# Attention of a hybrid decoder layer: heads in pairs, plain transposes, and the row sum divided out after the value product

## The chip, the cores and the metric

The kernel runs on one core of one Trainium2 chip. The metric is the device time of one execution, in microseconds (us). TensorE multiplies, VectorE (DVE), ScalarE (ACT) and GpSimd (POOL) do the element-wise work, SyncE (SP) issues most transfers.

## The reference

One decoder layer over 16 meta tokens and 1024 tokens of width 1024, all in float32. One input projection feeds two mixers: group A, eight heads of 64 channels with sparse attention, and group B, four heads of gated DeltaNet. Both outputs are gated, concatenated and projected into the residual. The part that the change touches is the attention of group A:

```python
idx_score = jnp.where(causal[None], idx_score, -jnp.inf)
_, sel = lax.top_k(idx_score, topk)               # 256 keys of each query
...
bias = rel_table[_t5_bucket(q_pos[None, :, None] - sel)]
logits = (jnp.einsum('bqhd,bqkhd->bqhk', qb, kg).astype(jnp.float32) * scale
          + jnp.moveaxis(bias, -1, 2).astype(jnp.float32))
logits = jnp.where(valid[:, :, None, :], logits, -jnp.inf)
p = jax.nn.softmax(logits, axis=-1).astype(vg.dtype)
return jnp.einsum('bqhk,bqkhd->bqhd', p, vg)
...
o_attn = _dsa_mixer(...) * jax.nn.silu(z_attn)
```

The kernel doesn't gather: it adds -1e30 to the logits of keys that aren't selected.

## The kernel before

It is written without a scheduler: each engine has its own program, and the engines meet only at semaphores. The stages, in time: projections and norms to about 100 us, index scores to 129, key/query norms and gates to 294, and the convolution's projections on TensorE to 462, while VectorE searches the top 256 keys until 490. Then comes the attention, from 495.8 to about 869, and last the DeltaNet with the output projection (L1453 to L1546; the first L1546 starts at 969 us), to the end of the span.

The attention works through 8 blocks `i` of 128 queries and, in each, 8 heads; `n = 8 i + h` counts them to 64. Block `i` has `KEYS[i] = 16 + 128 (i + 1)` keys, in `i + 2` tiles (tile 0 holds the 16 meta tokens). A head passes through:

- `dots(n)`, L1387 (and L1392 for the meta keys of the last block): queries times keys. Head `h` lies on rows 0 to 63 of the array when it is even and on rows 64 to 127 when it is odd. The logits go to one of two regions of three PSUM banks.
- `logits(n)`, L1028 to L1042 on VectorE: adds the penalty (far keys, L1033) or penalty and bias (near keys, L1039; the sum is prepared on GpSimd, L573), takes the row maximum, and negates it (L1042).
- `probabilities(n)`, L763 on ScalarE: the exponential in place, with its row sum.
- `sums(n)`, L1068 and L1070 on VectorE: the reciprocal of the row sum, and the identity scaled by it, a diagonal matrix.
- `turn_p(n)`, L1405: each tile of probabilities is multiplied by the diagonal as an ordinary matmul, which turns and normalises it. `copy_round` (L342 to L344) brings rounds of up to four tiles to SBUF, on VectorE and ScalarE by turns.
- `weigh(n)`, L1417: values (64 columns, stationary) times turned probabilities, summed over the tiles in bank 5. An even head fills PSUM partitions 0 to 63, an odd head 64 to 127.
- `gate_block(i)`, L1061: after eight heads, the output times the gate `zA`.

TensorE's order is `dots(n)`, `turn_p(n - 2)`, `weigh(n - 3)`; from n = 26 on, every third head is followed by L1433, eight products with one output column each, that sum squares for the DeltaNet (nine times). VectorE's order is `logits(m)`, `sums(m - 1)`, even copies of `m - 2` in the first 32 heads, and with `logits` after the copies in the last 32. A float32 matmul shows as two records in the trace, a float32 transpose (`turn(...)`, as in L1453) as one.

## Time and profile before

| | |
|---|---|
| runs | 1250.92 us median of 3 (1238.6 to 1269.38) |
| profiled execution, span | 1265.9 us; its time outside the span isn't listed |
| TensorE busy | 1155.0 us, 91% |
| VectorE busy | 722.8 us, 57% |
| ScalarE busy | 400.4 us, 32% |
| GpSimd busy | 237.3 us, 19% |
| mean granted clock of TensorE | 0.867 of full speed |
| HBM traffic | 36 GB/s over the span, up to 131 GB/s in a fortieth of it |

Busy time is what an engine spent in its instructions. TensorE's instructions overlap in the array, so its busy time says where it had work, not how fast it was; the spacing of its records says that. A granted clock of 0.50 is 1.2 GHz, 1.00 is 2.4 GHz.

### The profile page before, as it was taken

To read this page: it belongs to the slowest core of one execution; us is meant where nothing else is said; L and a number is where in the kernel's file an instruction comes from. 1 tells how busy PE (TensorE), PEld (TensorE's weight loads), DVE (VectorE), ACT (ScalarE), POOL (GpSimd) and SP (SyncE) were. 2 spreads that over 40 slices of the span, in tenths; PEclk is the share of its full clock that TensorE was granted. 3 is DMA by queue.
4 is the path that set the end of the run, shared out by engine and by line. 5 is a ranking of instruction groups with operands and counts; after the bars stand their busy time and mean duration, and the time that the engine had idled before them with its cause. 6 is when DMAs were issued, how large, how long until landed. Compare 5 with 4: busy or idle time off the path is not lost.

```text
span 1265.9 us, 14746 instructions
## 1 busy us (share of the span) xinstructions
PE 1155.0 (91%) x5008; PEld 762.5 (60%) x5008; DVE 722.8 (57%) x1767; ACT 400.4 (32%) x1237; POOL 237.3 (19%) x257
## 2 busy tenths in 40 slices
PE   6998999989999962999999999996869989999897
PEld 2544344445666631556677776775858867777754
DVE  2436898889999998443334434545365454644422
ACT  3425576694555512311112222332021210300200
POOL 5000000001545511111122121102123031221210
PEclk9989899999999985555569879999577979979999
DMA  4310303002011003000000000002000101101110
GB/s 131 128 49 1 124 26 100 33 17 84 1 67 39 28 1 116 17 12 6 17 1 18 17 1 17 10 1 75 1 1 1 50 1 50 50 1 50 50 50 34
DMA packets 26706, 46.75 MB, mean 37 GB/s; under 512 B 3408, under 2 KB 10864, under 8 KB 26640
## 3 DMA queue, kind: packets, MB, share of 16 engines
q1 hardware_dynamic: 26096, 45.78, 10.7%
q8 instruction: 40, 0.66, 0.2%
q0 software_dynamic: 544, 0.10, 0.2%
q14 instruction: 26, 0.21, 0.1%
HBM read 33.82 MB, written 12.05 MB: 36 GB/s over the span
## 4 chain that ended last, share of the span: by engine, by line
PE 61%; DVE 19%; issue 17%; ACT 2%; SPq 1%; DMA 0%; DVEq 0%; POOL 0%; POOLq 0%
PE ps L1405 10%; PE ps L1417 9%; PE ps L1546 8%; PE ps L1387 8%; PE ps L1252 5%; PE ps L1479 3%; DVE junk L961 3%; PE ps L1490 3%; DVE scores L1154 2%; PE ps L1482 2%; PE ps L1302 2%; PE ps L1433 1%; PE ps L1459 1%; DVE iw L956 1%; DVE iw L971 1%
## 5 line engine op out<-in xcount | busy, mean ns | idle before, releaser
L961 DVE TENSOR_SCALAR_CACHE_REDUCE junk<-scores,iw 128x272 bf16<-128x272 f32 (+6 forms) x224 | 200.6, 896 | 8.0
L1372 PE MATMUL ps<-areaH,areaW 128*128 128x384 f32 (+1 forms) x576 | 168.1, 455 | 1.6 <-ACT areaQ L721 1.6
L1372 PEld LDWEIGHTS ps<-areaH,areaW 128*128 128x128 f32 x576 | 109.4, 190 | 59.9 <-issue 1.8
L1387 PE MATMUL ps<-areaQ 64*128 64x512 f32 (+3 forms) x208 | 105.5, 632 | 34.4 <-ACT areaC L743 33.3
L1405 PE MATMUL ps<-areaH 128*128 128x128 f32 (+1 forms) x704 | 133.1, 340 | 1.3 <-DVE areaH L1070 0.8
L1405 PEld LDWEIGHTS ps<-areaH 128*128 128x128 f32 (+1 forms) x704 | 96.6, 211 | 49.6 <-issue 41.4
L1417 PE MATMUL ps<-areaH,areaQ 128*64 128x128 f32 (+1 forms) x704 | 123.8, 325 | 0.0
L1546 PE MATMUL ps<-areaW,areaQ 128*128 128x512 f32 x256 | 119.7, 613 | 1.7 <-DVE areaQ L1220 1.1
L1417 PEld LDWEIGHTS ps<-areaH,areaQ 128*64 128x64 f32 (+1 forms) x704 | 88.0, 159 | 27.1 <-issue 23.4
L763 ACT ACTIVATE areaH<-areaH,small 128x144 f32<-128x144 f32 (+7 forms) x64 | 50.5, 788 | 154.7 <-DVE small L1042 154.7
L557 POOL TENSOR_TENSOR staging<-staging,areaC 128x520 f32<-128x520 f32 x60 | 75.1, 1285 | 70.4 <-ACT areaC L757 70.4
L1387 PEld LDWEIGHTS ps<-areaQ 64*128 64x128 f32 x208 | 43.1, 239 | 73.3 <-issue 36.6
L573 POOL TENSOR_TENSOR areaH<-scores,tmp 128x256 f32<-128x256 f32 (+1 forms) x64 | 44.5, 696 | 227.0 <-DVE small L1039 221.9
L1546 PEld LDWEIGHTS ps<-areaW,areaQ 128*128 128x128 f32 x256 | 48.4, 198 | 51.6 <-issue 49.9
L1033 DVE CUSTOM_DVE_ANT_0 areaH<-ps,scores 128x16 f32<-128x16 f32 (+5 forms) x48 | 23.8, 497 | 76.6 <-PE ps L1387 76.6
L1252 PE MATMUL ps<-areaW,areaH 128*128 128x460 f32 (+1 forms) x144 | 59.8, 570 | 5.1 <-DMA areaW<-in_w_in 5.1
L811 ACT COPY scores<-ps 128x128 f32<-128x128 f32 x35 | 9.3, 266 | 166.2 <-PE ps L1479 166.2
L1350 PE MATMUL ps<-areaH,areaW 128*128 128x512 f32 x128 | 56.3, 594 | 0.0
L1350 PE MATMUL ps<-areaW,areaH 128*128 128x512 f32 x128 | 56.2, 592 | 0.0
L342 DVE COPY areaH<-ps 16x128 f32<-16x128 f32 x48 | 13.3, 278 | 71.7 <-PE ps L1405 71.3
L344 ACT COPY areaH<-ps 128x128 f32<-128x128 f32 (+3 forms) x40 | 17.0, 426 | 110.7 <-PE ps L1405 107.6
L757 ACT ACTIVATE areaC<-areaC,small 128x520 f32<-128x520 f32 x60 | 42.5, 723 | 24.3 <-POOL staging L557 24.3
(250 smaller groups left out, 1803.4 us busy)
## 6 DMA issues: line engine op xcount, KB each, us to landing
areaW<-in_w_in SPq DMA_DIRECT2D x5, 2048.0 KB, 8.8
areaC<-in_x SPq DMA_DIRECT2D x8, 512.0 KB, 3.5
areaW<-in_w_out SPq DMA_DIRECT2D x2, 2048.0 KB, 8.1
areaQ<-in_x SPq DMA_DIRECT2D x8, 512.0 KB, 5.1
y<-areaQ SPq DMA_DIRECT2D x8, 512.0 KB, 2.6
gate_a_scratch<-staging SPq DMA_DIRECT2D x8, 256.0 KB, 2.3
gate_g_scratch<-staging SPq DMA_DIRECT2D x8, 256.0 KB, 2.0
areaH<-gate_a_scratch SPq DMA_DIRECT2D x8, 256.0 KB, 2.9
```

The costliest lines, as they stand in the source:

```text
L557: nc.gpsimd.tensor_tensor(sums, sums, prod, ALU.add).then_inc(s_cvP, 1)
L573: nc.gpsimd.tensor_tensor(mbn[:, n % 2, 0:near], scores[:, SC0[i + 1] - near:SC0[i + 1]], bias[:, h, 256 - near:256], ALU.add).then_inc(s_ ...
L757: A(half(k)[1], conv[:, m, lo:lo + H2], ACT.Copy, scale=cw[:, 1 + k // 2, m:m + 1]).then_inc(s_prod, 1)
L763: A(L[:, n % 3, 0:nk], L[:, n % 3, 0:nk], ACT.Exp, bias=nm[:, n:n + 1], accum_out=rs[:, n:n + 1]).then_inc(s_P, 1)
L961: V.tensor_scalar(junk[:, 0:KEYS[i]], scores[:, SC0[i]:SC0[i] + KEYS[i]], patf[:, i - 1:i], 0.0, ALU.is_ge, ALU.add, accum_out=cnt[:, i - ...
L1252: ins = mm(ps[0:n, b, 0:NA], hT[:, k, tok(t)], wslot[:, 0, k, 0:NA], start=k == 0, stop=k == KD - 1)
L1350: ins = mm(ps[:, 2 + n % 2, :], w, hh, start=k == 0, stop=k == KD - 1)
L1372: ins = mm(ps[:, n % 4, 0:hi - lo], wslot[:, g % 2, k, 128 * m:128 * m + 128], hT[:, k, lo:hi], start=k == 0, stop=k == KD - 1)
L1387: ins = mm(pf[:, 1536 * (n % 2) + lo:1536 * (n % 2) + hi], qT[r, h // 2, 128 * i:128 * i + 128], kT[r, h // 2, lo0 + lo:lo0 + hi], start=T ...
L1405: ins = mm(ps[0:ROWS[kt], 6 + rr % 2, 128 * j:128 * j + 128], L[:, n % 3, tok(kt)], diag[:, n % 2, :], start=True, stop=True)
L1417: ins = mm(o, vN[0:ROWS[kt], kt, DA * h:DA * h + DA], pT[0:ROWS[kt], n % 2, kt, :], start=kt == 0, stop=kt == i + 1)
L1546: ins = mm(ps[:, 6 + q // 2, :], y, wslot[:, q // 2, k, :], start=k == 0, stop=k == 7)
```

## The change

- `dots(p)` computes a pair of heads (an even one and the next) in one step; the matmuls of the two row halves alternate. Each head writes its own two PSUM banks; up to 400 keys two pairs alternate inside them, above that the next pair waits until VectorE has read all of this one.
- Penalties, bias and queries are negated, so that the row minimum is the exponential's bias as it stands: the negation (L1042) is gone.
- `turn_p` becomes `turn_group`: a plain transpose against the identity, up to four tiles of the pair at a time, two pairs after `dots`. Value products follow two groups later, alternating between the pair's column halves. Groups, sums of squares and some small products share a ring of banks 5 to 7.
- `sums` is gone. Once per block, one reciprocal takes eight row sums, `scale_rows(i)` spreads them over 128 partitions with eight small matmuls, and VectorE multiplies the gate by them; `gate_block(i)` multiplies as before.
- The second half of the output weights (`load_group(7)`) is loaded after the attention, since its place holds four of the attention's buffers.

```diff
-        L = a.take(3, T)
-        pT = a.take(2, NT, 128)
+        L = a.take(6, T)
+        pT = a.take(4, 4, 128)
+        a = Area(areaW[:, KD * 512:2 * KD * 512])
         sqk = a.take(D)
-        mbn = a.take(2, 256)
+        mbn = a.take(4, 256)
         zA = a.take(2, 512)
-        diag = a.take(2, 128)
+        Lm = a.take(HA, META)
...
+        NP = HA * NB // 2
+        HP = HA // 2
+        LAG = 2
+
+        def tiles_of(i):
+
+            full = [(par, kt) for kt in range(1, i + 2) for par in range(2)] + [(0, 0), (1, 0)]
+            return [full[j:j + 4] for j in range(0, len(full), 4)]
+
+        GRP = [(p, tiles) for p in range(NP) for tiles in tiles_of(p // HP)]
+        G0 = [sum(len(tiles_of(q // HP)) for q in range(p)) for p in range(NP + 1)]
+        SQP = 13
+
+        def ring_steps():
+
+            by_step, nxt = [], 0
+            for st in range(NP + LAG):
+                now = []
+                if st == HP * (NB - 1):
+                    now += [("meta", 0, "D"), ("meta", 1, "D")]
+                if SQP <= st < SQP + NT:
+                    now.append(("ssq", st - SQP, "D"))
+                if st >= LAG:
+                    p = st - LAG
+                    for k in range(G0[p], G0[p + 1]):
+                        now.append(("turn", k, "DA"[nxt % 2]))
+                        nxt += 1
+                    if p % HP == HP - 1:
+                        now.append(("scale", p // HP, "D"))
+                by_step.append(now)
+            return by_step
+
+        RING = ring_steps()
+        FLAT = [e for now in RING for e in now]
+        AT_RING = {e[:2]: c for c, e in enumerate(FLAT)}
...
+        def ring_bank(c):
+            return 5 + c % 3
...
+        def logit_base(p):
+
+            return 512 * (p % 2) if KEYS[p // HP] <= 512 else 0
...
-            load_group(7)
+            sp.wait_ge(s_ch, 36)
...
+            load_group(7)
...
-                A(L[:, n % 3, 0:nk], L[:, n % 3, 0:nk], ACT.Exp, bias=nm[:, n:n + 1],
+                nk, buf = KEYS[n // HA], 2 * (n // 2 % 3) + n % 2
+                act.wait_ge(s_red, n + 1)
+                A(L[:, buf, 0:nk], L[:, buf, 0:nk], ACT.Exp, bias=mx[:, n, 1:2], scale=-1.0,
...
+                else:
+                    dve.wait_ge(s_za[k % 2], 16 * (k // 2 + 1))
+                    V.tensor_tensor(zA[:, k % 2, :], bank, zA[:, k % 2, :], ALU.mult).then_inc(s_rd, 1)
...
+            for step in range(NP + LAG):
+                ops = logit_ops(step) if step < NP else []
+                if ops:
+                    dve.wait_ge(s_S, step + 1)
+                    if step >= 3:
+                        dve.wait_ge(s_ring, AT_RING["turn", G0[step - 2] - 1] + 1)
...
+                if step >= LAG and (step - LAG) % HP == HP - 1:
+                    i = (step - LAG) // HP
+                    dve.wait_ge(s_P, HA * (i + 1))
+                    V.reciprocal(rinv[:, i % 2, :], rs[:, HA * i:HA * i + HA]).then_inc(s_ri, 1)
+                if ops:
+                    logits(*ops.pop(0))
+                for what, k, who in RING[step]:
+                    if who == "D" and what != "meta":
+                        read_ring(what, k)
+                    if what == "turn" and k in GATE_AT:
+                        gate_block(GATE_AT[k])
+                    if ops:
+                        logits(*ops.pop(0))
+                while ops:
+                    logits(*ops.pop(0))
+                if 1 <= step < CONV:
+                    conv_tap(11, step)
...
+            def fill(what, k):
+                c = AT_RING[what, k]
+                if c >= 3:
+                    pe.wait_ge(*ring_read(c - 3))
+                return ring_bank(c)
+
+            def dots(p):
+                i, g = p // HP, p % HP
+                lo0, base = split(i), logit_base(p)
+                if KEYS[i] > 512 and p:
+                    pe.wait_ge(s_red, 2 * p)
+                elif p >= 2:
+                    pe.wait_ge(s_red, 2 * (p - 1))
                 for lo, hi in pieces(KEYS[i] - lo0):
-                    ins = mm(pf[:, 1536 * (n % 2) + lo:1536 * (n % 2) + hi], qT[r, h // 2, 128 * i:128 * i + 128],
-                             kT[r, h // 2, lo0 + lo:lo0 + hi], start=True, stop=True)
-                if lo0:
-                    if h:
-                        pe.wait_ge(s_meta, h)
-                    ins = mm(ps[:, 2, 0:META], qT[r, h // 2, 128 * i:128 * i + 128], kT[r, h // 2, 0:META],
+                    for par in range(2):
+                        r = slice(64 * par, 64 * par + 64)
+                        ins = mm(pf[:, 1024 * par + base + lo:1024 * par + base + hi],
+                                 qT[r, g, 128 * i:128 * i + 128], kT[r, g, lo0 + lo:lo0 + hi], start=True, stop=True)
+                ins.then_inc(s_S, 1)
+
...
-                ins.then_inc(s_S, 1)
-
-            def turn_p(n):
-
-                i = n // HA
-                pe.wait_ge(s_dg, n + 1)
-                for r, tiles in enumerate(rounds(i)):
-                    rr = ROUND0[n] + r
-                    if rr >= 2:
-                        pe.wait_ge(*turned(rr - 2))
-                    for j, kt in enumerate(tiles):
-                        ins = mm(ps[0:ROWS[kt], 6 + rr % 2, 128 * j:128 * j + 128], L[:, n % 3, tok(kt)],
-                                 diag[:, n % 2, :], start=True, stop=True)
-                    ins.then_inc(s_PT, 1)
-
-            def weigh(n):
-                i, h = n // HA, n % HA
-                if h == 0 and i:
+                ins.then_inc(s_ring, 1)
+
+            def turn_group(k):
+
+                p, tiles = GRP[k]
+                pe.wait_ge(s_P, 2 * (p + 1))
+                b = fill("turn", k)
+                for j, (par, kt) in enumerate(tiles):
+                    ins = turn(ps[0:ROWS[kt], b, 128 * j:128 * j + 128], L[:, 2 * (p % 3) + par, tok(kt)], ident)
+                ins.then_inc(s_ring, 1)
+
+            def weigh(k):
+                p, tiles = GRP[k]
+                i, g = p // HP, p % HP
+                if i and k == G0[HP * i]:
                     pe.wait_ge(s_on, i)
-                for r, tiles in enumerate(rounds(i)):
-                    pe.wait_ge(*turned(ROUND0[n] + r))
-                    for kt in tiles:
-                        o = ps[DA * (h % 2):DA * (h % 2) + DA, 5, 128 * (h // 2):128 * (h // 2) + 128]
-                        ins = mm(o, vN[0:ROWS[kt], kt, DA * h:DA * h + DA], pT[0:ROWS[kt], n % 2, kt, :],
-                                 start=kt == 0, stop=kt == i + 1)
+                pe.wait_ge(*ring_read(AT_RING["turn", k]))
+                for j, (par, kt) in enumerate(tiles):
+                    h = 2 * g + par
+                    ins = mm(ps[DA * par:DA * par + DA, 4, 128 * g:128 * g + 128],
+                             vN[0:ROWS[kt], kt, DA * h:DA * h + DA], pT[0:ROWS[kt], k % 4, j, :],
+                             start=kt == 1, stop=kt == 0)
                 ins.then_inc(s_o, 1)
 
-            for n in range(HA * NB + 3):
-                if n < HA * NB:
-                    dots(n)
-                if 2 <= n < HA * NB + 2:
-                    turn_p(n - 2)
-                if n >= 3:
-                    weigh(n - 3)
...
+            def scale_rows(i):
+
+                pe.wait_ge(s_ri, i + 1)
+                b = fill("scale", i)
+                for g in range(HP):
+                    for par in range(2):
+                        h = 2 * g + par
+                        ins = mm(ps[DA * par:DA * par + DA, b, 128 * g:128 * g + 128],
+                                 rinv[:, i % 2, h:h + 1].broadcast_to([128, DA]), ident, start=True, stop=True)
+                ins.then_inc(s_ring, 1)
+
+            for step in range(NP + LAG):
+                for what, k, _ in RING[step]:
+                    if what == "meta":
+                        dots_meta(k)
+                if step < NP:
+                    dots(step)
+                for what, k, _ in RING[step]:
+                    if what == "ssq":
+                        sum_squares(k)
+                    elif what == "turn":
+                        turn_group(k)
+                        if k >= 2:
+                            weigh(k - 2)
+                    elif what == "scale":
+                        scale_rows(k)
+            for k in range(len(GRP) - 2, len(GRP)):
+                weigh(k)
```

## Rows read from the trace of the kernel before

**Rows 1.** The page's section 4, the chain that ended last, by engine and line.

```profile
PE 61%; DVE 19%; issue 17%; ACT 2%; SPq 1%; DMA 0%; DVEq 0%; POOL 0%; POOLq 0%
PE ps L1405 10%; PE ps L1417 9%; PE ps L1546 8%; PE ps L1387 8%; PE ps L1252 5%; PE ps L1479 3%; DVE junk L961 3%; PE ps L1490 3%; DVE scores L1154 2%; PE ps L1482 2%; PE ps L1302 2%; PE ps L1433 1%; PE ps L1459 1%; DVE iw L956 1%; DVE iw L971 1%
```

**Rows 2.** Windows of 20 us in the attention: busy of each engine, granted clock.

```profile
core 0: us, PE busy (x) PEld busy (x) DVE busy (x) ACT busy (x) POOL busy (x), PEclk, DMA share, GB/s
...
600.00:620.00 20.00, 20.00 (x79) 12.91 (x78) 6.89 (x27) 3.10 (x10) 3.80 (x4) 0.50 0.08 27
...
640.00:660.00 20.00, 20.00 (x98) 14.60 (x98) 7.60 (x29) 3.28 (x9) 5.33 (x5) 0.76 0.00 1
...
820.00:840.00 20.00, 20.00 (x127) 14.83 (x127) 10.31 (x34) 6.14 (x13) 2.15 (x4) 1.00 0.04 15
```

**Rows 3.** The chain in order of time, blocks 2 to 4: start, duration, engine, line, records.

```profile
598.13 2.12 PE ps L1405 x8
600.25 2.09 PE ps L1417 x8
602.33 2.24 PE ps L1387 x4
...
625.71 2.54 PE ps L1405 x10
...
658.61 2.45 PE ps L1387 x4
```

**Rows 4.** The same chain, blocks 5 to 7.

```profile
724.23 1.86 PE ps L1405 x14
726.09 1.81 PE ps L1417 x14
...
773.48 2.08 PE ps L1405 x16
775.56 2.03 PE ps L1417 x16
...
846.76 1.91 PE ps L1387 x4
```

**Rows 5.** The same chain: sums of squares, and sixteen transposes at two moments.

```profile
638.07 3.50 PE ps L1433 x16
...
748.46 1.88 PE ps L1433 x16
...
927.29 2.29 PE ps L1453 x16
...
1002.66 1.77 PE ps L1453 x16
```

**Rows 6.** TensorE's timeline, index products of the last block, heads on alternate row halves.

```profile
122.85 3.08 PE L1302 MATMUL ps<-areaC 64*128 64x512 f32 x12 [0.20 <-ACT tmp L684]
126.08 3.08 PE L1302 MATMUL ps<-areaC 64*128 64x512 f32 x12 [0.16 <-ACT tmp L684]
```

**Rows 7.** Groups by line on VectorE: busy us, mean ns, idle before.

```profile
L1070 DVE TENSOR_SCALAR areaH<-small 128x128 f32<-128x128 f32 x64 | 25.6, 399 | 2.2
...
L1068 DVE RECIPROCAL small<-small 128x1 f32<-128x1 f32 x64 | 10.4, 163 | 32.2 <-ACT areaH L763 30.3 <-issue 1.1 <-DVE scalars L1104 0.7
...
L1042 DVE TENSOR_SCALAR small<-small 128x1 f32<-128x1 f32 x64 | 9.8, 154 | 2.2
```

**Rows 8.** Timeline of one head of block 7, on VectorE and ScalarE.

```profile
843.43 0.53 DVE L343 COPY areaH<-ps 128x384 f32<-128x384 f32 x1
844.12 0.59 ACT L344 COPY areaH<-ps 128x512 f32<-128x512 f32 x1 [2.83 <-PE ps L1405]
...
844.96 1.02 DVE L1033 CUSTOM_DVE_ANT_0 areaH<-ps,scores,small 128x768 f32<-128x768 f32 x1
...
846.02 0.48 DVE L1039 CUSTOM_DVE_ANT_0 areaH<-ps,areaH,small 128x256 f32<-128x256 f32 x1
...
846.74 1.16 ACT L763 ACTIVATE areaH<-areaH,small 128x1040 f32<-128x1040 f32 x1 [2.04 <-DVE small L1042]
```

More of the change, by code:

```diff
@@ L346, in hybrid @@
-        ROUND0 = [0]
-        for i in range(NB):
-            for h in range(HA):
-                ROUND0.append(ROUND0[-1] + len(rounds(i)))
-        def turned(r):
-            return ((s_PTe, r // 2 + 1) if r % 2 == 0 else (s_PTa, r // 2 + 1))
+        NP = HA * NB // 2
[4 more added lines that the diff above has]
+            return [full[j:j + 4] for j in range(0, len(full), 4)]
@@ new lines, in hybrid, with ring_read, copy_group @@
+        RING = ring_steps()
+        FLAT = [e for now in RING for e in now]
+        AT_RING = {e[:2]: c for c, e in enumerate(FLAT)}
+        def ring_read(c):
+            who = FLAT[c][2]
+            return (s_rd if who == "D" else s_ra), sum(e[2] == who for e in FLAT[:c + 1])
+        def ring_bank(c):
+            return 5 + c % 3
+        def copy_group(copy, k):
+            p, tiles = GRP[k]
+            src = ps[:, ring_bank(AT_RING["turn", k]), :].rearrange("p (k t) -> p k t", k=4)
+            nf, m = sum(kt > 0 for _, kt in tiles), len(tiles)
+            if nf:
+                ins = copy(pT[:, k % 4, 0:nf, :], src[:, 0:nf, :])
+            if m > nf:
+                ins = copy(pT[0:META, k % 4, nf:m, :], src[0:META, nf:m, :])
+            return ins
@@ new lines, in logits @@
+            def logits(what, n, buf, far, lo0, at):
+                i, p = n // HA, n // 2
+                if what == "far":
+                    first = -LOWEST
+                    if lo0:
+                        V.tensor_tensor_reduce(L[:, buf, 0:lo0], Lm[:, n % HA, :], scores[:, SC0[i]:SC0[i] + lo0],
+                                               1.0, first, ALU.add, ALU.min, mx[:, n, 1:2]).then_inc(s_meta, 1)
+                        dve.wait_ge(s_meta, n % HA + 1)
+                        first = mx[:, n, 1:2]
+                    V.tensor_tensor_reduce(L[:, buf, lo0:far], pf[:, at:at + far - lo0],
+                                           scores[:, SC0[i] + lo0:SC0[i] + far],
+                                           1.0, first, ALU.add, ALU.min, mx[:, n, 0:1]).then_inc(s_far, 1)
+                    return
+                first, near = -LOWEST, KEYS[i] - far
@@ L1072, in _ @@
[L1072 to L1091 removed]
+                V.tensor_tensor(oA, ps[:, 4, :], zA[:, i % 2, :], ALU.mult).then_inc(s_on, 1)
@@ L1100, in _ @@
                     assert g[0] == G_CB, g
-                if m == SQ0 + 3 * NT + 8:
+                if step == SQP + NT + 4:
                     dve.wait_ge(s_ga, 8)
                     glink(V.tensor_scalar(skbe, skbe, -1.0, None, ALU.mult))
+            gate_block(NB - 1)
             glink(V.memset(AT[0], 0.0))
@@ L1421, in _ @@
[L1421 to L1435 removed]
+            def fill(what, k):
+                c = AT_RING[what, k]
+                if c >= 3:
+                    pe.wait_ge(*ring_read(c - 3))
+                return ring_bank(c)
@@ new lines, in sum_squares @@
+            def sum_squares(t):
+                pe.wait_ge(s_sqk, t + 1)
+                b = fill("ssq", t)
+                for j in range(8):
+                    ins = mm(ps[0:ROWS[t], b, j:j + 1], sqk[:, 128 * j:128 * j + ROWS[t]], ones[:, 0:1],
+                             start=True, stop=True)
+                ins.then_inc(s_ring, 1)
+            def scale_rows(i):
+                pe.wait_ge(s_ri, i + 1)
+                b = fill("scale", i)
+                for g in range(HP):
+                    for par in range(2):
+                        h = 2 * g + par
+                        ins = mm(ps[DA * par:DA * par + DA, b, 128 * g:128 * g + 128],
+                                 rinv[:, i % 2, h:h + 1].broadcast_to([128, DA]), ident, start=True, stop=True)
+                ins.then_inc(s_ring, 1)
@@ new lines, in _ @@
+            for step in range(NP + LAG):
+                for what, k, _ in RING[step]:
[12 more added lines that the diff above has]
+                        scale_rows(k)
```

204 lines of the change are left out of this document (79 added, 125 removed).

## The prediction, made before the changed kernel ran

> **What bounds the kernel now.** Read the chain that ended last first [rows 1]. Three lines of the attention hold 27% of it: L1405 (turning the probabilities) 10%, L1417 (value products) 9%, L1387 (query times key) 8%. Of the span of 1265.9 us that is 342 us, nearly the whole stage, which runs from 495.8 us to about 869 us: 373 us. So TensorE sets its length. The windows say the same [rows 2]: TensorE is busy 20.00 us of 20 at 600, 640 and 820 us, while VectorE has 6.89, 7.60 and 10.31. They also show that the granted clock is 0.50 at 600 us (1.2 GHz), 0.76 at 640, and 1.00 (2.4 GHz) at 820. Every term below therefore has two prices, a low and a high one.
>
> **Prices.** In the chain at the low level a round of 10 records at L1405 takes 2.54 us and one of 8 takes 2.12 us [rows 3]: 0.21 us a record. 8 x 0.21 = 1.68, so 0.44 us is left over, for two changes of the shape in the array: onto this line, and from the 16-column meta tile to the full ones. L1417 (2.09 for 8) is alike. At the high level 16 records take 2.08 and 14 take 1.86, at L1417 2.03 and 1.81 [rows 4]: 0.11 us a record, and 0.3 us left over. I use 0.2 us for a change at the low level and 0.15 us at the high. `dots` takes 2.45 us for 656 keys at the low level [rows 3], 3.7 ns a key, and 1.91 us for 1024 at the high one [rows 4], 1.9 ns a key, its change included. 528 keys take 2.24 at the low level, since short pieces don't pay; I keep that.
>
> **The change, part by part.**
>
> *Plain transposes.* Sixteen transposes, one record each, take 1.77 us in the DeltaNet [rows 5]: 0.11 us each at the high level. A turned tile costs two records at L1405 now, and one afterwards. There are 8 x 44 = 352 tiles. This is the surest part: 352 x 0.11 = 39 us at the high level, 74 us at the low one.
>
> *Pairs on both row halves.* The trace has a place where heads on opposite halves follow each other without a long wait, the index products. There two heads with the largest number of keys take 3.08 us, and the next two start 3.23 us after the first [rows 6]: 1.6 us a head, less than the 1.91 us of the same 1024 keys alone [rows 4]. Halves do overlap, though there a semaphore holds the second head back for a part. Bounds for a pair: twice a head (no overlap) and one head. I take one head: the code alternates the halves at every piece, and rows 6 show overlap under a worse order.
>
> *Value products by column halves.* `weigh` now alternates between output partitions 0 to 63 and 64 to 127. No row shows two column halves following each other, since a head's products all use one half. Bounds: no gain, and one half free. The nearest row is that of the row halves, so I take the half; this is the weakest term, and the main rival prices the other end. A loss is bounded by the shape changes, which are counted.
>
> The Trainium skill (TensorEngine Tiling, When to Use Tiling) says that a stationary operand of up to 64 columns can be column-tiled twofold; by it the half is right, and no row here shows it.
>
> *Shape changes.* Value products now come in 32 pairs' groups of four, each between two turns: 1, 2, 2, 3, 3, 4, 4, 5 groups a pair in blocks 0 to 7. With the meta tiles these are 4, 4, 6, 6, 8, 8, 10, 10 changes a pair beside that in `dots`.
>
> *Sum per pair.* dots + 2(i+2) records of turns + 2(i+2) of value products (half of 4(i+2)) + changes. Low level, blocks 0 to 7: 3.0, 4.3, 6.1, 7.6, 9.1, 10.4, 12.1, 13.5 us; block 3 is 2.24 + 20 x 0.21 + 6 x 0.2. High level, blocks 3 to 7: 4.1, 5.1, 5.8, 6.7, 7.4 us; block 7 is 1.95 + 36 x 0.11 + 10 x 0.15.
>
> *Which level.* The clock is at its low level at 600 us, changes in the window from 640 us (the fourth block), and is at the high level at 820 us [rows 2]. The L1433 group, eight products of one column, costs 1.88 us at the high level [rows 5], and the `dots` behind it run slowly for some us. Nine such groups stay, now one behind each `dots` of steps 13 to 21, in blocks 3 to 5. I take blocks 0 to 2 at the low level, 3 to 5 half way, 6 and 7 high: 4 x 13.4 = 54, 4 x (5.9 + 7.1 + 8.1) = 84, 4 x 14.1 = 56; together 194 us.
>
> *What is added.* Nine L1433 groups between 1.88 and 3.50 us [rows 5], 2.4 each: 22 us, as before. `scale_rows`: eight products a block, 16 records, in column halves, with its changes 1.3 us: 10 us. The first value product of a block waits for `gate_block` (one half of a bank each, some 0.7 us and the way there); behind it on TensorE stand all later turns, and behind those ScalarE's exponentials: 7 x 1 us. Its own wait is new in one respect: VectorE must have read the scaled gate first, which it did a step earlier. Filling and draining, two pairs deep: 5 us. Sum 238 us.
>
> *VectorE.* It loses L1042, L1068 and L1070, 45.8 us [rows 7], all of it off the path; their worth is room. It gets 8 reciprocals and 8 gate products. In block 7 a head costs it 1.02 + 0.48 us for logits and about 0.53 us for each of its copies [rows 8]; from the 10.31 us in 20 us, near three heads, less 3 x 0.6 us, a pair is left with 5.7 us against TensorE's 7.4 us. That fits, but above 512 keys `dots` of a pair waits for the last reduction of the one before, which stands behind this pair's ring copies: about 2 us of `dots`, then 4 ops and two copies, 4 to 5 us, beside 5.4 us of turns and products. Bounds: nothing, and 1 us a pair in blocks 4 to 7, 16 us. I take nothing. ScalarE (1.16 us per exponential, 0.59 us per copy) and GpSimd stay below both.
>
> *The moved load.* `load_group(7)` is 2 MB that was issued at the start of the attention; now it is issued at the end of it. Its reader is the first output product, L1546, which starts 100 us after the attention. Nothing, then; without that cover it would cost its own duration, at most the 16 us that 2 MB take at 130 GB/s, the most that the kernel moves anywhere. On SP's queue it is now ahead of the DeltaNet's first tiles (gate, attention output, residual), whose first reader is GpSimd in the stage `w`; I take nothing, and the same 16 us as the upper bound.
>
> **Result.** 373 - 238 = 135 us less: 1265.9 - 135 = 1131 us for a profiled span. The median of the runs, 1250.92, is 15 us below that span, and the range of those runs is 31 us wide. 1251 - 135 = **1116 us**.
>
> **Rivals.**
>
> *Value products don't overlap.* For it: no row shows that they do. Then 4 pairs x 2(i+2) records come back: 72 x 0.21 in blocks 0 to 2, 144 x 0.16 in 3 to 5, 136 x 0.11 in 6 and 7 (15 + 23 + 15), and 4 us in `scale_rows`: 57 us more, **1173**.
>
> *No halves overlap.* Against it stand rows 6. `dots` twice: 43 us more, **1216**.
>
> *The level stays low, halves overlap.* The transposes' share of TensorE's records grows, and groups are cut up by changes. Blocks 3 to 5 cost 24 us more, 6 and 7 46 us, L1433 10 us: 80 us more, **1196**. Against it: at 927 us sixteen transposes took 2.29 us, at 1002 us 1.77 us [rows 5]; 2.29 lies between sixteen at 0.21 and at 0.11, so the level rose inside a run of them.
>
> The Trainium skill (TensorE: Matmul & The Clock Gate, Part 4) holds that transposes don't count as activity for the clock gate and the full level doesn't engage in them. By that rule this rival, or the next, would be the likely one; the trace agrees only in so far as the low level is common where TensorE's work is cut up, and rows 5 speak against it.
>
> *Slower.* The level stays low through the whole stage and the value products run one after the other: the added 57 us at low prices are 77, so the stage is 238 + 80 + 77 = 395 us, 22 us more than now: **1273**; with serial `dots` too, about **1338**. It decides from where the stage costs more than 373 us: with all terms at the low level, a quarter of the column overlap missing in half the blocks doesn't suffice; nearly all of it must be missing.
>
> *Better.* The pairs' dense `dots` bring the high level in block 1 or 2, and L1433 doesn't take it away: up to 42 us less, say **1080**.
>
> **Chances.** Forecast 0.45; value products serial 0.24; low level 0.09; no overlap 0.08; better 0.09; slower 0.05. A change below 2% (25 us) can't be told from none here. From the cases: faster 0.89, same 0.06, slower 0.05. The range runs from 1085, most of "better", to 1200, past "serial" and "low level"; outside lie no overlap, slower and a part of better.
>
> **What the changed profile would show.** Turns: one record a tile, 0.21 or 0.11 us apart. `dots`: about 2 us for a pair of 1040 keys at the high level, not 3.9. Value products: eight records of a group in 0.45 us, not 0.9, at the high level. The windows of blocks 6 and 7: clock near 1.00, TensorE busy throughout, VectorE near 15 of 20 us. If TensorE idles there, released by VectorE's L1039, the reduction's wait was mispriced. If the DeltaNet stage isn't about 397 us long, something moved that I priced at nothing. The prediction falls with the column halves or with the clock.

## The result, and the profile after

The changed kernel takes **1097.89 us**, the median of 4 runs (1074.72 to 1112.72). Run beside it, the kernel before takes 1260.15 us, the median of 4 (1238.6 to 1274.26). The ratio is **0.8745**, with a 95% interval of 0.8602 to 0.8889. The profiled execution of the changed kernel is the longest of its four: 1112.72 us, with a span of 1111.0 us. The forecast was a ratio of 1116 / 1251 = 0.892. (Ratios here and below use only executions within 1.5% of the fastest of their kernel beside it, so they aren't the quotients of the medians; both profiled executions, before and after, are longer than that.)

Where did the time go? The windows over the two stages answer first. Columns: window; its length, then the busy us (and instructions) of PE, PEld, DVE, ACT and POOL; granted clock; DMA share; GB/s. The attention and the DeltaNet stage of the changed kernel:

```profile
494.20:708.30 214.10, 203.31 (x1569) 129.65 (x1569) 107.09 (x357) 83.67 (x198) 61.22 (x73) 0.82 0.07 22
708.30:1111.00 402.70, 355.10 (x1848) 279.82 (x1848) 179.56 (x351) 61.16 (x220) 77.52 (x67) 0.84 0.10 37
```

The same two of the kernel before:

```profile
495.80:869.10 373.30, 369.45 (x1793) 249.31 (x1793) 155.50 (x576) 88.64 (x210) 59.63 (x73) 0.75 0.05 18
869.10:1265.90 396.80, 347.27 (x1848) 273.46 (x1848) 181.22 (x351) 61.16 (x220) 77.53 (x67) 0.86 0.10 32
```

The attention is 159 us shorter, 214 us instead of 373 us. It has 224 TensorE records fewer (352 for the second record of each turned tile, less 128 for `scale_rows`), but 166 us less TensorE time. So most of the gain is not a smaller count; the records that are left start closer together, partly since they overlap and partly since the clock is higher: the mean granted clock rose from 0.75 to 0.82. The DeltaNet stage is 6 us longer with the same number of instructions on every engine, at a lower clock (0.84 instead of 0.86).

The chain that ended last, by engine and by line (it answers to [rows 1]; L1471 turns, L1482 is the value product, L1453 is `dots`):

```profile
PE 54%; DVE 22%; issue 20%; ACT 2%; SPq 1%; DMA 1%; DVEq 0%; POOL 0%; POOLq 0%
PE ps L1633 10%; PE ps L1482 5%; PE ps L1311 5%; PE ps L1471 5%; PE ps L1453 4%; PE ps L1566 3%; PE ps L1577 3%; DVE junk L998 3%; DVE scores L1213 2%; PE ps L1569 2%; PE ps L1361 2%; PE ps L1491 2%; PE ps L1546 1%; DVE iw L993 1%; DVE iw L1008 1%
```

The three lines of the attention that held 27% now hold 14%, in a shorter span. The sums of squares, L1491, have 2% of it, where they had 1% [rows 1].

TensorE's timeline in the last block (start, us, engine, line, operation, shapes, count, and in brackets the idle time before it and who ended it). It answers to the high-level blocks of [rows 4]:

```profile
676.68 1.99 PE L1453 MATMUL ps<-areaQ 64*128 64x512 f32 x8
678.60 0.66 PE L1471 MATMUL ps<-small,areaH 128*128 128x128 f32 x4
679.19 0.66 PE L1482 MATMUL ps<-areaH,areaQ 128*64 128x128 f32 x8
679.78 0.66 PE L1471 MATMUL ps<-small,areaH 128*128 128x128 f32 x4
...
682.38 0.66 PE L1482 MATMUL ps<-areaH,areaQ 128*64 128x128 f32 x8 [0.62 <-DVE staging L1117]
```

Eight records of `dots`, 2 x 1024 keys, take 1.99 us, where one head with 1024 keys took 1.91 us [rows 4]. Four turned tiles, starting at 678.60, hold the line until 679.19: 0.59 us. The eight value-product records behind them also hold it for 0.59 us. At [rows 4]'s 0.11 us a record, four and eight records one after another are 0.44 and 0.88 us, and each group has a change of shape. So the eight value products cost as much as four.

The middle of the stage looks different, here at 565 us:

```profile
562.59 2.54 PE L1453 MATMUL ps<-areaQ 64*128 64x512 f32 x8
565.05 1.95 PE L1491 MATMUL ps<-small,areaW 128*128 128x1 f32 x16
566.86 0.63 PE L1471 MATMUL ps<-small,areaH 128*128 128x128 f32 x4
...
573.43 3.57 PE L1491 MATMUL ps<-small,areaW 128*128 128x1 f32 x16
576.86 1.09 PE L1471 MATMUL ps<-small,areaH 128*128 128x128 f32 x4
577.89 1.12 PE L1482 MATMUL ps<-areaH,areaQ 128*64 128x128 f32 x8
```

The same kinds of group take 0.63 to 0.66 us at one moment and 1.09 to 1.12 us at another, behind an L1491 group that itself took 3.57 us. The windows show that this is the clock; their seventh column is to be read beside [rows 2]:

```profile
520.00:540.00 20.00, 19.86 (x186) 11.46 (x184) 14.23 (x63) 10.88 (x35) 8.85 (x13) 1.00 0.15 54
540.00:560.00 20.00, 19.73 (x138) 14.26 (x138) 7.58 (x30) 5.42 (x14) 9.04 (x8) 0.70 0.09 28
560.00:580.00 20.00, 20.00 (x113) 13.28 (x111) 5.86 (x22) 4.65 (x11) 6.92 (x8) 0.59 0.00 1
580.00:600.00 20.00, 19.79 (x149) 13.77 (x148) 8.51 (x27) 5.91 (x14) 6.88 (x7) 0.76 0.08 27
600.00:620.00 20.00, 20.00 (x126) 12.79 (x128) 6.72 (x23) 5.55 (x13) 6.05 (x7) 0.67 0.00 1
...
640.00:660.00 20.00, 19.79 (x180) 12.04 (x176) 14.31 (x40) 10.46 (x25) 4.65 (x7) 1.00 0.08 27
```

Before, the clock was at its low level (0.50, 1.2 GHz) at 600 us. Now it is at its high one (1.00, 2.4 GHz) at 520 us already, falls again and again between 540 and 620 us, where the nine L1491 groups stand (539.5 to 614.7 us), and stays high from 640 us to the stage's end.

### The profile page after: what moved, and what is told of

It reads as the page before. It is cut to its first block, busy times and chain, and to the rows that moved or that the text cites. A ratio compares the mean times of both kernels' runs of the same rounds, so it can differ in the third digit from the quotient of the medians.

```text
span 1111.0 us, 14013 instructions
## 1 busy us (share of the span) xinstructions
PE 994.7 (90%) x4784; PEld 648.3 (58%) x4784; DVE 673.0 (61%) x1548; ACT 395.5 (36%) x1225; POOL 239.0 (22%) x257
## 4 chain that ended last, share of the span: by engine, by line
PE 54%; DVE 22%; issue 20%; ACT 2%; SPq 1%; DMA 1%; DVEq 0%; POOL 0%; POOLq 0%
PE ps L1633 10%; PE ps L1482 5%; PE ps L1311 5%; PE ps L1471 5%; PE ps L1453 4%; PE ps L1566 3%; PE ps L1577 3%; DVE junk L998 3%; DVE scores L1213 2%; PE ps L1569 2%; PE ps L1361 2%; PE ps L1491 2%; PE ps L1546 1%; DVE iw L993 1%; DVE iw L1008 1%
## 5 line engine op out<-in xcount | busy, mean ns | idle before, releaser
L1453 PE MATMUL ps<-areaQ 64*128 64x512 f32 (+4 forms) x208 | 51.4, 611 | 35.1 <-ACT areaC L781 33.4
L1482 PE MATMUL ps<-areaH,areaQ 128*64 128x128 f32 (+1 forms) x704 | 69.8, 316 | 2.3 <-DVE staging L1117 1.5
L1471 PE MATMUL ps<-small,areaH 128*128 128x128 f32 (+1 forms) x352 | 65.9, 312 | 5.1 <-ACT areaH L801 5.0
L610 POOL TENSOR_TENSOR areaW<-scores,tmp 128x256 f32<-128x256 f32 (+1 forms) x64 | 46.0, 745 | 79.8 <-DVE small L1087 73.9
L1482 PEld LDWEIGHTS ps<-areaH,areaQ 128*64 128x64 f32 (+1 forms) x704 | 40.3, 149 | 27.2 <-issue 22.3
L1471 PEld LDWEIGHTS ps<-small,areaH 128*128 128x128 f32 (+1 forms) x352 | 38.1, 143 | 30.1 <-issue 16.6
L1453 PEld LDWEIGHTS ps<-areaQ 64*128 64x128 f32 x208 | 22.3, 237 | 55.9 <-ACT areaC L781 34.0
L383 ACT COPY areaH<-ps 128x512 f32<-128x512 f32 (+1 forms) x36 | 18.5, 514 | 102.0 <-PE ps L1471 102.0
L629 POOL TENSOR_TENSOR areaH<-areaH,masks 128x512 f32<-128x512 f32 x26 | 30.2, 1166 | 73.6 <-PE ps L1566 63.0
L1283 DVE TENSOR_TENSOR areaQ<-ps,areaQ 128x1024 f32<-128x1024 f32 x8 | 9.8, 1225 | 59.7 <-PE ps L1633 59.7
```

The source lines that it names most:

```text
L610: nc.gpsimd.tensor_tensor(mbn[:, 2 * (p % 2) + par, 0:near], scores[:, SC0[i + 1] - near:SC0[i + 1]], bias[:, 2 * g + par, 256 - near:256] ...
L1453: ins = mm(pf[:, 1024 * par + base + lo:1024 * par + base + hi], qT[r, g, 128 * i:128 * i + 128], kT[r, g, lo0 + lo:lo0 + hi], start=True, ...
L1471: ins = turn(ps[0:ROWS[kt], b, 128 * j:128 * j + 128], L[:, 2 * (p % 3) + par, tok(kt)], ident)
L1482: ins = mm(ps[DA * par:DA * par + DA, 4, 128 * g:128 * g + 128], vN[0:ROWS[kt], kt, DA * h:DA * h + DA], pT[0:ROWS[kt], k % 4, j, :], star ...
```

## The experiments

Attention lengths are from the start of the first `dots` to the start of the DeltaNet's first products, in the profiled execution; the clock beside each is the window's mean.

| kernel | median us (range) | attention us | clock |
|---|---|---|---|
| changed, run again | 1105.78 (1102.61 to 1107.54) | 202.6 | 0.87 |
| e1, one column half at a time | 1108.9 (1105.73 to 1114.42) | 216.8 | 0.92 |
| e2, `dots` head by head | 1093.87 (1089.8 to 1097.09) | 205.0 | 0.86 |
| e3, turned by a matmul | 1128.93 (1121.85 to 1138.17) | 236.9 | 0.93 |
| e4, before, with plain transposes | 1242.78 (1218.35 to 1250.77) | 325.5 | 0.72 |
| e5, an eighth of the square sums | 1075.22 (1070.94 to 1090.24) | 176.4 | 0.94 |
| e6, two groups at a time | 1080.41 (1078.91 to 1093.28) | 181.7 | 0.94 |
| e7, square sums by halves | 1083.05 (1074.47 to 1090.88) | 183.6 | 0.94 |
| e8, e6 and e7 | 1073.78 (1061.25 to 1085.33) | 176.9 | 0.93 |
| e9, `dots` on one row half | 1185.37 (1174.52 to 1202.44) | 296.4 | 0.68 |
| e10, VectorE work added | 1116.85 (1106.93 to 1120.29) | 209.4 | 0.85 |
| e11, e1, e3 and e9 | 1212.08 (1202.84 to 1217.59) | 311.7 | 0.87 |

Two things are needed to read this table. The rest of the span, whose code is the same in all versions of the changed kernel, took between 883 us (e3) and 909 us (e10) in these profiles, 903 us in the repeat. A total can therefore move by some 20 us with nothing changed outside the attention but the clock. And the changed kernel itself has eight executions, 1074.72 to 1112.72 us, of which two were profiled, with a whole-run clock of 0.889 and 0.892. Its two fastest had 0.925 and 0.912 and took 1074.72 and 1087.09 us; no profile shows where their clock was high. The medians of e5, e6 and e7 lie between these two.

**The changed kernel again.** Expected:

> The changed kernel unaltered, beside the three variants of it. Both theories: a ratio to the kernel before near 0.8745, so about 1098 us, with single runs between 1075 and 1113. What to read in its profile: how long the attention and the DeltaNet last (212 and 403 us in the first profile), and how much of the run-to-run spread lies in each.

Measured: 1105.78 us, ratio 0.8972 (0.8837 to 0.9106). Its attention is 11.5 us shorter than in the first profile. The same instructions ran; the clock differs (0.87 against 0.82). Two executions of one program can differ by this much, so a difference of 10 us in the attention means something only together with the clock.

**e1. One column half at a time.** All value products of the even head first, then those of the odd head:

```
full = [(par, kt) for par in range(2) for kt in range(1, i + 2)] + [(0, 0), (1, 0)]
```

> The value products of a pair are ordered head by head (all tiles of the even head, then all of the odd one, meta tiles last) instead of alternating. Same instructions, same groups of four. Theory (column halves run at the same time only when both have work queued): from block 3 on most groups hold one head alone, some 240 records of 0.11 to 0.21 us lose their cover: 30 to 45 us slower than the changed kernel, and a group of one head shows 8 records in about 0.9 us at the high level against 0.45. Rival (the value products got cheaper for another reason, order is no matter): within 10 us.

```profile
679.62 0.66 PE L1471 MATMUL ps<-small,areaH 128*128 128x128 f32 x4
680.20 1.09 PE L1482 MATMUL ps<-areaH,areaQ 128*64 128x128 f32 x8
681.22 0.39 PE L1471 MATMUL ps<-small,areaH 128*16 128x128 f32 x2
```

Eight records in one column half take 1.09 us where the alternating ones take 0.66 us. So column halves do overlap, and a group of eight saves 0.43 us at the high level. Yet the attention became only 14 us longer and the total 3 us (0.9019, 0.8863 to 0.9175), where 30 to 45 us were expected. (Not all value products are serial in e1: some groups still hold tiles of both heads.) What stage and total differ by lies outside the attention, where e1's profile is 16 us shorter than the repeat's with the same code. The windows of e1 say what happened inside it:

```profile
560.00:580.00 20.00, 20.00 (x146) 14.32 (x142) 7.42 (x26) 5.84 (x14) 6.93 (x7) 0.87 0.00 1
580.00:600.00 20.00, 19.79 (x158) 15.16 (x156) 9.63 (x33) 5.85 (x14) 9.10 (x9) 1.00 0.09 28
600.00:620.00 20.00, 19.80 (x160) 13.72 (x157) 9.25 (x28) 7.54 (x17) 4.88 (x7) 1.00 0.08 27
```

The clock that was 0.59, 0.76 and 0.67 there (0.58, 0.99 and 0.83 in the repeat) is 0.87, 1.00 and 1.00, with the same L1491 groups among the records. The slower products cost time; the higher clock gave a part of it back.

**e2. `dots` head by head.** The head's loop outside the pieces' loop, so that the halves don't alternate:

```
for par in range(2):
    for lo, hi in pieces(KEYS[i] - lo0):
```

> In dots the pieces of the even head come first, then those of the odd head; up to 512 keys nothing changes, above that the halves no longer alternate piece by piece. Theory A (only neighbours in the order overlap): a pair of 1040 keys goes from 1.9 us to about 3 us at the high level, 25 us in all. Theory B (each row half has its own line of work, as the index products let suspect, where the second head started while four records of the first were left): no change, within 8 us, and a pair still takes 1.9 us.

```profile
667.24 1.99 PE L1453 MATMUL ps<-areaQ 64*128 64x512 f32 x8
```

The pair takes 1.99 us in this order too, and the attention 2 us more than in the repeat. The total is 12 us below the repeat's, with intervals that overlap (0.8877, 0.8731 to 0.9024); the difference lies outside the attention. With four records of one half queued first, both halves still take little more than one. The alternation, on which the prediction rested, isn't what makes them overlap; using both halves is.

**e3 and e4. The transposes.** e3 puts the product with the unit matrix back into the changed kernel; e4 takes the kernel before and only makes its turns plain transposes (so it leaves the division by the row sum out):

```
-    ins = turn(ps[...], L[...], ident)
+    mm(ps[...], L[...], ident, start=True, stop=True)     # e3
-    mm(ps[...], L[...], diag[...])
+    ins = turn(ps[...], L[:, n % 3, tok(kt)], ident)      # e4
```

> The plain transposes are ordinary float32 matmuls with the identity, two records a tile instead of one; all else stays. Theory (the transposes saved 352 records): 352 x 0.11 to 0.21 us, about 50 us slower than the changed kernel. Rival (transposes leave the clock at its low level, matmuls would raise it): less than 20 us slower, with more of the stage at the high level, in blocks 3 to 5 above all.

> The kernel before with one part of the change: the turning matmuls (two records a tile) become plain transposes (one record). VectorE still makes the reciprocal and the diagonal and TensorE still waits for it, but the probabilities stay undivided: the division by the row sum is left out. Theory (352 records less on the bounding engine): 39 to 74 us less, about 55 us, ratio 0.955. Rival (the level of the clock falls when the transposes take the place of matmuls): under 30 us, with more of blocks 4 to 7 at the low level than the 64 us of before.

```profile
675.43 1.16 PE L1471 MATMUL ps<-small,areaH 128*128 128x128 f32 x8
676.52 0.80 PE L1483 MATMUL ps<-areaH,areaQ 128*64 128x128 f32 x8
```

In e3 a group of four tiles holds the line for 1.09 us, not 0.59. The 352 tiles are 88 times four, so 44 us at the high level; measured were 34 us more attention at a clock of 0.93 instead of 0.87, and 23 us more in total (0.9193, 0.9004 to 0.9382). In e4 the attention is 48 us shorter than before (325.5 against 373.3 us), at 0.72 against 0.75. But this sets the fastest of e4's four executions beside one of the longer ones of before. Between the medians e4 gained 24 us (1242.78 against 1266.96 us beside it), between the fastest executions 18 (1218.35 against 1236.49). So the 39 to 74 us of the prediction are right as a count of records, and both times the whole kernel moved by less. Both times the clock was lower with the transposes: 0.889 to 0.895 in the repeat's four executions against 0.910 to 0.924 in e3's, and 0.831 to 0.862 in e4's against 0.854 to 0.887 in those of before beside it. The rival of both expectations, that transposes leave the clock lower than matmuls do, is borne out in part.

**e5 and e7. The sums of squares.** e5 issues one product for eight (so seven of eight sums are left out). e7 keeps them all, but has each made for 64 tokens at a time, in alternate column halves:

```
-for j in range(8):
-    mm(ps[0:ROWS[t], b, j:j + 1], sqk[:, 128*j:128*j + ROWS[t]], ones[:, 0:1])
+for j in range(8):                                                       # e7
+    for lo in range(0, ROWS[t], 64):
+        w = min(64, ROWS[t] - lo)
+        mm(ps[lo:lo + w, b, j:j + 1], sqk[:, 128*j + lo:128*j + lo + w], ones[:, 0:1])
```

> The changed kernel, where each of the nine groups of eight one-column products is one product of eight columns: seven of the eight sums of squares are left out and the first one stands in their place. Directly 9 x 1.7 to 3.2 us go, some 20 us. Theory (these groups are also what takes the clock to its low level in blocks 3 to 5): 30 to 45 us less in the attention, with hardly any low level after its first 25 us. Rival (the level falls there for the cut-up work itself): about 20 us less and as much low level as before.

> The changed kernel, where each one-column product over 128 tokens is two over 64 tokens, alternating between the column halves: 32 records instead of 16 in a group. Theory (the time of these groups is that of loading 128 stationary columns per record, 0.117 us, and halves load at the same time): a group falls from 1.9 to about 1 us, 9 to 15 us less in all, and some of the low level goes too. Rival (a fixed cost per record, or loads that don't overlap): a group stays at 1.9 us or grows towards 3.8 us.

One group of e7, and then its clock where the changed kernel had 0.59:

```profile
550.52 1.10 PE L1493 MATMUL ps<-small,areaW 128*64 128x1 f32 x32
```

```profile
560.00:580.00 20.00, 19.79 (x258) 13.59 (x256) 10.51 (x36) 8.64 (x21) 10.12 (x10) 1.00 0.10 28
```

Twice the records take 1.10 us, not 1.95. The first of the nine groups, that of the 16 meta tokens, takes 0.55 us in both; eight groups with 0.85 us less each are 7 us. In e5 one of the eight holds the line for 0.24 us instead of about 1.9, so 13 us in all. But against the repeat of the changed kernel the attention is 19 us shorter in e7 and 26 us in e5: 12 to 13 us more than the count in both, and in both the clock is 1.00 in every window from 520 us to the stage's end. So the level doesn't fall when the L1491 groups are short. That they alone take it away is not shown: e1 and e3 keep them as they are and lose the level there for some 10 us in all, by their windows, and e6 below for less. And since the changed kernel's faster executions weren't profiled, how much of the 12 to 13 us is the edit and how much the execution stays open.

**e6. Two groups at a time.** Turned groups are weighed in twos, so that there are about half as many changes of shape:

```
-if k >= 2: weigh(k - 2)
+if k >= 3 and k % 2: weigh(k - 3); weigh(k - 2)
```

> The changed kernel with two groups turned, then two groups of value products, instead of one and one: half of the 2 x 96 changes between transposes and value products go. Theory (a change costs 0.15 to 0.2 us of its own on TensorE): 96 x 0.15 = 14 us less or somewhat more, if nothing else ends the wait. Rival (VectorE and ScalarE now set the pace of the ring of three banks): no gain, TensorE idles at the transposes for a bank instead.

```profile
657.02 1.09 PE L1482 MATMUL ps<-areaH,areaQ 128*64 128x128 f32 x16
658.04 1.09 PE L1471 MATMUL ps<-small,areaH 128*128 128x128 f32 x8
```

Sixteen value records hold the line for 1.02 us where two groups of eight held it for 2 x 0.59 = 1.18, and eight turns for 1.03. So a change of shape costs about 0.15 us at the high level, as estimated. Its attention is 21 us shorter than that of the repeat, where 14 us were expected, part of it again by the clock (0.94 against 0.87). This kernel keeps all nine groups of square sums at their full length, one here and then the clock behind it:

```profile
557.10 1.95 PE L1491 MATMUL ps<-small,areaW 128*128 128x1 f32 x16
```

```profile
540.00:560.00 20.00, 19.12 (x146) 14.88 (x148) 8.11 (x29) 4.43 (x11) 7.50 (x8) 0.83 0.09 29
560.00:580.00 20.00, 19.39 (x188) 14.89 (x189) 10.68 (x38) 8.35 (x19) 10.73 (x10) 1.00 0.09 27
580.00:600.00 20.00, 20.00 (x192) 14.41 (x191) 10.50 (x33) 8.20 (x19) 7.50 (x10) 1.00 0.01 2
```

So these groups don't bring the level down by themselves: in the changed kernel the level falls where they stand for some 50 us in all; here, with coarser groups around them, for some 7 us.

**e8. Both.** e6 and e7 together:

> The changed kernel with both edits that gained alone: two groups turned, then two groups of value products, and the sums of squares by column halves. Theory (the one takes changes of shape out, the other the slow one-column groups; both also keep the clock high): the gains add up only in part, since each alone already left just 22 to 23 us at the low level: about 170 us of attention, 1065 to 1070 us. Rival (both gain through the same low-level time, nothing else): 1075 to 1083 us, as each alone.

Measured: **1073.78 us, ratio 0.8631 (0.8527 to 0.8735)**, the lowest median of the study. All six executions are shorter than the repeat's four, but the interval overlaps that of the changed kernel's first measurement (0.8602 to 0.8889), and e8's executions (1061.25 to 1085.33 us) overlap those of e5, e6 and e7. The attention is 176.9 us, only 5 to 7 us less than with either edit alone. Either edit alone is already at a clock of 0.94, and that can be gained only once.

**e9. `dots` on one row half.** `r = slice(0, 64)` for both heads (so the odd head's scores are those of the even head):

> The changed kernel, where the odd head's logits are computed from rows 0 to 63, too: the odd head uses the even head's queries and keys, so its part is left out. Same instructions, but both heads of a pair on one row half. Theory (the pair's halves run at the same time): a pair of 1040 keys takes about 3.9 us at the high level against 1.9, 36 us more over the stage at the high level, less what a better filled TensorE gains from the clock: 20 to 43 us slower. Rival (the halves don't matter, the matmuls of a pair overlap anyway): within 8 us.

```profile
751.93 3.70 PE L1453 MATMUL ps<-areaQ 64*128 64x512 f32 x8
```

```profile
520.00:540.00 20.00, 20.00 (x82) 10.53 (x79) 7.76 (x33) 4.98 (x17) 5.62 (x8) 0.50 0.08 27
540.00:560.00 20.00, 20.00 (x85) 10.63 (x83) 7.55 (x30) 3.90 (x13) 3.80 (x6) 0.50 0.08 27
...
680.00:700.00 20.00, 20.00 (x102) 13.67 (x100) 5.70 (x17) 3.35 (x8) 1.41 (x2) 0.61 0.00 1
```

A pair takes 3.70 us instead of 1.99. Priced like that, serial `dots` were 43 us in the prediction. Measured are 80 us in the median (0.9569, 0.9427 to 0.9712) and 94 us in the attention of the profiled execution, which is the longest of its four. TensorE is busy 20.00 us of 20 at all three places, but the clock is 0.50 from 500 to 620 us, where the changed kernel has 1.00 at 520 us. So by the prediction's count about half of what the row halves bring comes through the clock. This is the largest single effect of the study. That serial `dots` keep the level low is not a rule, though: e11 has them too, and a clock of 1.00 at 540 us.

**e10. VectorE work added.** A scaling of a 128x128 tile behind each near reduction:

```
+V.tensor_scalar(spare, ident, 1.0, None, ALU.mult)
```

> The changed kernel with one more VectorE instruction a head, a scaled copy of the 128x128 identity to a spare place behind each last reduction, like the diagonal of before (64 x 0.4 us = 26 us of VectorE). Theory (VectorE has room; what was taken from it was worth nothing by itself): less than 6 us slower. Rival (in the new stage VectorE's chain of logits and ring copies ends last): 15 to 26 us slower.

VectorE got 15 us more work, so 0.24 us each. The attention is 7 us longer than in the repeat (209.4 against 202.6 us), the median 11 us. But from the start of the last square sums to the stage's end, where the last ten pairs lie, it takes 95.8 us against 95.5 us. The 7 us fall in the earlier part, where the clock moves too; that a little of them is VectorE's stays open. In these last pairs, where VectorE has most to do, more work on it costs nothing.

**e11. Three savings undone.** e1, e3 and e9 in one kernel (the odd head's scores again those of the even head):

> The changed kernel with all three of TensorE's savings undone at once: both heads' logits from rows 0 to 63 (the odd head uses the even head's queries and keys), turning by two-record matmuls, value products head by head. Pairs, ring, lag and the later division stay. Theory (the three savings are the whole gain and each is worth more while the clock is low): about the time of the kernel before, 1250 to 1280 us. Rival 1 (the savings add up as measured one by one, 80 + 23 + 3 us above the changed kernel): about 1212 us, so that 50 us come from the new order itself. Rival 2 (a TensorE that has more to do keeps the high level, as with each of the two smaller edits): 1190 us or less.

Measured: 1212.08 us, ratio 0.9543 (0.9484 to 0.9602). The single effects add up to 3 + 23 + 80 = 106 us, and 1105.8 + 106 = 1212 us. That the sum fits is luck: in the attention the single effects are 14 + 34 + 94 = 142 us and all three together 109 us. On top of serial `dots`, undoing the other two costs 15 us there (311.7 against 296.4 us in e9), since the clock rises from 0.68 to 0.87. Without overlap in either direction and with two records a tile, the kernel is still 57 us faster than before (1268.63 us beside it), and its attention takes 312 us, not 373. Its windows show a clock of 1.00 at 540 us and a mean of 0.87 over the stage, against 0.75. How much of these 60 us is the new order (longer runs, one ring, two pairs of lag) in itself and how much the clock was not split further.

## Why the prediction came out

**Right: what bounds the stage.** TensorE set its length before and does now, 203 of 214 us. From 640 to 700 us it is busy 19.2 to 19.8 us of 20 and VectorE 10.9 to 14.3, below the 15 that were foreseen.

**Right: the transposes.** One record a tile, 352 records less; 44 us by e3's group, 48 us by e4's stage, against 39 to 74. What the prediction left out is the clock, which was lower with them in both comparisons: the whole kernel moved by 23 us in e3 and 24 us in e4.

**Right, by a wrong reason: the row halves.** A pair costs 1.99 us as forecast. "The code alternates the halves at every piece" was the argument, and e2 shows that the order doesn't matter.

**Right: the column halves**, "the weakest term". Groups of eight take the time of four (0.59 us); the rival that forecast 1173 falls with e1's trace. Its price of 57 us was not measured, since e1 makes only a part of the products serial. For that part 30 to 45 us were expected at a fixed clock, and the stage took 14 us more. The Trainium skill (TensorEngine Tiling, When to Use Tiling) gives twofold column tiling for a stationary operand of up to 64 columns; the trace agrees.

**Mis-sized: "Which level".** This is the step that failed by size: blocks 0 to 2 were put at the low level, 54 us, with 5 us for filling. From the first `dots` to the first square sums (539.5 us) the stage takes 45 us. That stretch holds blocks 0 to 2 up to the last pair's turns, the `dots` of two pairs of block 3, and a wait near its start that had not been foreseen:

```profile
507.23 1.11 PE L1471 MATMUL ps<-small,areaH 128*128 128x128 f32 x4 [5.04 <-ACT areaH L801]
```

```profile
503.36 1.07 ACT L773 ACTIVATE areaC<-staging 128x1040 f32<-128x1040 f32 x1 [3.36 <-DVE staging L1044]
504.45 1.28 ACT L807 ACT_TABLE_LOAD   x1
```

TensorE waits 5 us for an exponential of the third pair. ScalarE has done those of the first two pairs and then stands 3.36 us behind VectorE's last pieces of the convolution (L1044), takes their output (L773) and loads its table for the exponential again. From then on the high level comes within the first blocks: the "better" rival's first half. Its second half, that the level then stays, is wrong: blocks 3 to 5 are at 0.59 to 0.76 in four of the windows, near the half way that was forecast. The whole stage was forecast at 238 us and took 214 and 203 us in two executions. So the total came out partly by luck: the clock of the early blocks was put too low, and how long the later ones run at the high level differs from execution to execution.

**Fell: "the level stays low".** From 620 to 700 us the clock is 0.93 to 1.00, and of the records from 676 us on about three in ten are transposes. The Trainium skill (TensorE: Matmul & The Clock Gate, Part 4) holds that transposes don't count as activity and don't bring the full level. The trace shows that the full level holds with transposes standing between matmuls; what transposes alone would do no run here shows, and e3 and e4, with the lower clock on the side of the transposes, lean towards the page. The level fell where the one-column products stand, but e6 has the same products without the fall, so what exactly brings it down stays open.

**Right: the waits.** A block's first value product waits 0.62 us for `gate_block`; forecast 1 us. `scale_rows` holds the line for 0.97 us (675.71 to 676.68) at the high level; forecast 1.3. The wait for VectorE's reductions in `dots`, taken at nothing, comes to less than 1 us from 512 us to the stage's end.

**Not shown to cost: the moved load.** The DeltaNet stage took 402.7 us against 396.8. In the other kernels, with the same code there, it took 390 to 406 us, 390 with a clock of 0.88 and 406 with 0.83. The 6 us lie within that.

**Where the sum landed.** 135 us less were forecast, 162 us were measured between the medians and 155 us between the profiled spans (1265.9 and 1111.0 us). Of the 20 us between 135 and 155, the stage gives 24 (238 against 214) and the stretch ahead of it 2, and the DeltaNet's 6 us go the other way. The last 7 us are only the distance of the two profiled executions from their medians.

## What to carry to other kernels

An edit on TensorE is priced twice: by its records at the present clock, and by what it does to the clock. Putting both row halves to work saved 43 us by count and 80 in fact; making value products slower cost 14 us in the stage where 30 to 45 were expected. So read the stage and its clock beside every total, and profile more than one execution before a clock is put down to an edit. Where the windows show a lower clock, fewer changes of shape (e6) or shorter one-column groups (e7) are worth a trial; such gains don't add, as e8 shows.

## What the runs showed of the hardware

- Halves of the array overlap without alternation: 1.99 us for a pair of 1024 keys, whether the pieces alternate or one half's four records are queued first.
- Column halves overlap even with 128 moving columns: eight records take 0.66 us, and 1.09 us in one half. Sixteen records with one moving column take 1.95 us; the same sums as 32 records in alternate halves take 1.10 us.
- The busy share doesn't tell the clock: at 20.00 us busy of 20 the granted clock was 0.50 in e9 (520 us) and 1.00 in e11 (540 us), and at 19.86 us it was 1.00 in the changed kernel (520 us). What does tell it, these runs don't show.
- Less work at the same place can mean a lower clock: the changed kernel's attention ran at 0.82 and 0.87, e1 and e3, with more records or slower ones, at 0.92 and 0.93, and e11 at 0.87 where e9 had 0.68.
- With plain transposes the whole-run clock was lower than with matmuls in their place: 0.889 to 0.895 against 0.910 to 0.924 (repeat and e3), 0.831 to 0.862 against 0.854 to 0.887 (e4 and before). Beside this stands the spread of one kernel: the changed kernel's first four executions had 0.889 to 0.925.
